# Opening the program with the input projection, and dealing page compression's other products out between its chunks

## The chip, the cores and the metric

One core of one Trainium2 chip runs the whole program. The metric is the device time of one execution in microseconds (us), the median over several runs. TensorE (PE in the profile) multiplies; VectorE (DVE), ScalarE (ACT) and GpSimd (POOL) work on elements; SyncE (SP) and the queues of the other engines start DMA transfers. The five engines run their own instruction streams and meet at semaphores. TensorE's clock has two levels, 2.4 GHz (granted clock 1.00 in the profile) and 1.2 GHz (0.50).

## The reference

One inference step of a two-layer decoder, for a prompt of 512 tokens and 8 single sample tokens together (T = 520 columns everywhere, D = 1024). Layer 0 mixes tokens with native sparse attention, layer 1 with a gated linear recurrence; each layer ends in a SwiGLU network. The part that matters here is how layer 0 begins:

```
q, kv, gates = split(rms_norm(x) @ nsa_w_in)          # 1024 -> 2608 columns
z  = blocks of 64 raw K (or V) rows + position weights # prompt: 8 blocks, sample: 8 x 32 blocks from paged cache
kc = silu(z @ w1) @ w2                                  # 4096 -> 64 -> 64 for each block and head
s_c = q . kc * scale + bias(distance)                   # scores of the prompt over its 8 blocks, softmax
```

The distance bias is one table of 32 buckets x 16 heads, looked up by token distance.

## The kernel before

All products are in float32 or in pairs of rounded parts: a weight tile and an activation are each cut into a high part and a rest, and three products take the place of one. `linear` (L137) runs a projection over weight tiles of 512 KB that lie in a ring of four slots. For each tile ACT copies the high part (`cut`, L280), DVE subtracts it (L312), PE does 8 x 6 matmuls of 260 columns (`one`, L400), and DVE moves the result out of one of four PSUM banks. In the first tile PE also adds up the squares of x (L413) for the RMS norm, whose inverse root is wanted before the first result moves out: two-bank lookahead lets PE do tile 1 meanwhile, and it waits for the inverse before tile 2. SP loads tile n+4 when the rest of tile n is cut, and after each of the first 16 such loads runs `beside`, which fetches two pages of the compression cache (`first_chunks`). The projection has 21 tiles.

Ahead of it stands a block of its own, `bias_rows` (L1154). SP loads the one-hot rows, the table, x in one piece, small constants, and the first four weight tiles; PE makes the 16 x 1024 bias rows with two float32 matmuls (L1188); DVE scales them; ACT stores them to DRAM. A block ends for all engines together, and SP ends it only when x and the constants are in. Then the projection's block starts. There SP first runs `early` (`spread_bias`, L2596): it waits for the stored rows and copies them 128 times with a shift, 5 MB within DRAM, in one transfer.

Page compression is the block `compress` (L1199). The cache's 128 pages are taken as 8 chunks of 16 pages, 256 KB each, in two slots of 4 MB. Chunks 0 and 1 are in when the block starts. Chunk g+2 goes into the slot of chunk g: SP (9 pages) and POOL (7 pages) wait for `chunk_done` of chunk g and then issue the page loads one after another (`load_chunk`, L1250). A chunk is 128 float32 matmuls of 64 columns on 64-column weights (L1295), each two records in the trace. Beside the chunks PE has other products here: turning gates and values (L1327, L1330, L1310), the prompt's blocks against w1 (`prompt`, L1303, 17 columns, 2 x 128 records), the block bias (L1339, 14 matmuls of 16 columns), the second products (L1347, L1349, at the end L1381 and L1384), the block scores (L1361, 32 matmuls of 16 columns on 128-column weights), the turned probabilities (L1368) and the sample bias (`far`, L1318, six). The order on PE is written out by hand: chunk 0, 1, gates, new values, both prompt products, block bias, values of two tiles, chunk 2, second products and the other values, chunk 3, all block scores, chunk 4, turned probabilities, far 0 and 1, chunk 5, far 2 and 3, chunk 6, far 4 and 5, chunk 7, the last second products. The attention block follows.

Later, between the first network and the recurrence's projection, ACT takes the last inverse root of the norm (`end.root(act, 4, ...)`, L542, at the end of `Layer.scalar`), then cuts the high part of tile 2 (L280). DVE waits for the root (`rooted`), cuts the rest (L312), and moves tile 0 out (L2071), which frees the bank that tile 2 needs.

Of the kernel before, what the change touches and what calls it, by code (L numbers as in the profile page):

```python
# [20 lines left out]
P = 128  # L21
# [30 lines left out]
SKEW = SEQ + P  # L52
FINE = (0, 1, 2, 4, 8, 16)
# [83 lines left out]
def linear(c, name, w, n_units, subs, kcs, src, evac, nxt, scale=None, beside=None, norm=None, early=None, late=None, work=None, unrolled=False, first=None, start=0):  # L137
# [19 lines left out]
    with ExitStack() as ctx:  # L157
# [19 lines left out]
        def rounds(eng, cut, first_done=None, tail=None):  # L177

            def step(i, s):
                if cut is not None:  # L180
                    cut(i, s)
                if isinstance(i, int) and i == 0 and s == 0:
                    if first_done is not None:
                        first_done()
                    return
                if isinstance(i, int) and i == 0 and s == 1 and tail is not None and norm is not None:
                    tail()
                r, q = (i, s - 1) if s else (i - 1, RING - 1)
                if q % subs == subs - 1:
                    evac(eng, ps, q // subs, r, ready)  # L190

# [51 lines left out]
        def _(sp):  # L243
            if first is not None:
# [31 lines left out]
        def _(act):  # L276
# [5 lines left out]
            def cut_source():  # L282
                if post is not None:
                    root(1)
                for k in range(kcs):
                    if post is not None:
                        act.wait_ge(x_new[k % 2], k // 2 + 1)
                    act.activation(xh[:, k, :], src[:, k, :], ACT.Copy,
# [9 lines left out]

            if first is not None:
# [71 lines left out]
        def _(pool):  # L371
            if post is not None:
# [9 lines left out]
        def _(pe):  # L382
# [33 lines left out]
            def add_squares(k):  # L416
                pe.wait_ge(squared, k + 1)
                token_sums(ps[2], sq[:, k % 2, :], k == 0, k == kcs - 1).then_inc(added, 1)
# [189 lines left out]
class Layer:  # L608
# [108 lines left out]
    def scalar(self, act):  # L717
# [101 lines left out]
        end.root(act, 4, COLS[1])  # L819
# [13 lines left out]
    def vector(self, dve):  # L833
# [97 lines left out]
        end.mean(dve, own_end, 1)  # L931

# [221 lines left out]
def bias_rows(c, d, tabs, oh, R, loaded, row_out):  # L1154

    nc = c.nc
    with ExitStack() as ctx:
        ps = [ctx.enter_context(nc.psum_tensor(f"row_ps{j}", [P, 512], F32)) for j in range(2)]
        made, moved = [nc.alloc_semaphore(f"row_{n}") for n in ("products", "scaled")]
        oh_in = nc.alloc_semaphore("row_onehot_loaded")  # L1160
        block = ctx.enter_context(nc.Block())

        @block.sync
        def _(sp):
            sp.dma_start(oh, d["onehot_rows"][:, 0]).then_inc(oh_in, 16)
            sp.dma_start(tabs[:, :], d["tabs"]).then_inc(oh_in, 16)
            for dst, src in loaded[1]:
                sp.dma_start(dst, d[src]).then_inc(loaded[0], 16)
            for s in range(RING):
                load_tile(sp, c, d["nsa_w_in"], s, s, KC)  # L1170
            sp.wait_ge(loaded[0], 16 * len(loaded[1]))

        @block.scalar
        def _(act):
            act.wait_ge(moved, 2)
            act.dma_start(d["bias_scratch"], R).then_inc(row_out, 16)

        @block.gpsimd
        def _(pool):
            pool.memset(c.ones[:, :], 1.0)  # L1180
            for s in range(RING):
                pool.sem_inc(c.psum_free[s], 1)

        @block.tensor
        def _(pe):
            pe.wait_ge(oh_in, 32)
            for j in range(2):
                pe.matmul(ps[j][0:16, :], tabs[:, 0:16], oh[:, j * 512:(j + 1) * 512], start=True, stop=True)\  # L1188
                  .then_inc(made, 1)

        @block.vector
        def _(dve):
            for j in range(2):
                dve.wait_ge(made, j + 1)
                dve.tensor_scalar(R[:, j * 512:(j + 1) * 512], ps[j][0:16, :], HD ** 0.5, None, ALU.mult).then_inc(moved, 1)


def compress(c, d, at, tabs, first_in, w1, w1_in, kcBD, v_rep, skew_out):
# [7 lines left out]
    with ExitStack() as ctx:  # L1206
# [47 lines left out]
        def _(sp):  # L1254
# [17 lines left out]
            sp.wait_ge(skew_out, 16)  # L1272
# [11 lines left out]
        def _(pe):  # L1284
            def chunk(g):
# [11 lines left out]
                mm.then_inc(chunk_done[s], 1)  # L1297
# [9 lines left out]
            def values(i, bank):  # L1307

                for j, u in enumerate((SV_U, SV_U + 1, WV_U, WV_U + 1)):
                    mm = pe.transpose(bank[:, j * P:(j + 1) * P], HT[:, u, i * P:(i + 1) * P], c.ident[:, :])  # L1310
                mm.then_inc(tok_turned, 1)
# [8 lines left out]

            pe.wait_ge(w1_in, 16)
            pe.wait_ge(first_in, 16 * 2 * CH)
            chunk(0)
            chunk(1)
# [10 lines left out]
            pe.wait_ge(onehots, 32)  # L1335
            for x in range(PBLK + 2 * (TILES - 1)):

                first = BLOCK * (2 * (TILES - 1) - x) - (BLOCK - 1) + 511
                mm = pe.matmul(b[2][:, x * 16:(x + 1) * 16], oh[:, first:first + P], tabs[:, 0:16], start=True, stop=True)  # L1339
            mm.then_inc(blocks_biased, 1)  # L1340
            values(0, b[5])
            pe.wait_ge(gates_out, 1)
            values(1, b[3])
            chunk(2)
# [6 lines left out]
            pe.wait_ge(new_out, 1)  # L1351
            values(2, b[4])
            pe.wait_ge(tok_out, 1)
            values(3, b[5])
            chunk(3)
            pe.wait_ge(bias_out, 1)
            pe.wait_ge(kc_ready, 1)
            for i in range(TILES):
                for u in range(8):
                    col = (i * 8 + u) * 16  # L1360
                    mm = pe.matmul(b[2][:, col:col + 16], c.XW[:, u, i * P:(i + 1) * P],  # L1361
                                   kcBD[:, u // REP].rearrange("p g n -> p (g n)"), start=True, stop=True)
            mm.then_inc(scores, 1)
            chunk(4)
            pe.wait_ge(probs, 1)
            pe.wait_ge(tok_out, 4)
# [4 lines left out]
            far(0)  # L1371
            far(1)
            chunk(5)
            far(2)
            far(3)
            chunk(6)
            far(4)
            far(5)
            chunk(7)
# [8 lines left out]
        def _(act):  # L1388
# [9 lines left out]
            for j, (first, n) in enumerate(FAR):  # L1398
                act.wait_ge(far_biased, j + 1)
                act.activation(at.bias[:, first:first + n], b[4 + j % 2][:, 0:n], ACT.Copy).then_inc(far_out, 1)  # L1400
            for s in range(2):
                act.wait_ge(chunk_done[s], NCH // 2)
            for kv in range(2):
                act.activation(hid[:, kv, 0:512], ps_c[kv][:, :], ACT.Silu, bias=pe_w[:, kv:kv + 1]).then_inc(hidden, 1)

# [1137 lines left out]
def program(nc, d):  # L2543

    with ExitStack() as top:
# [19 lines left out]
        with ExitStack() as nsa:  # L2565
# [12 lines left out]
            bias_rows(c, d, tabs, carve(HT[0:N_BUCKETS + 1, 4:6, :].rearrange("p u t -> p (u t)"), 0, 1024),  # L2578
                      carve(HT[0:16, 11:13, :].rearrange("p u t -> p (u t)"), 0, 1024),
# [180 lines left out]
```

## Time and profile before

| | |
|---|---|
| median of 3 runs | 1723.29 us (1721.01 to 1731.25) |
| the profiled execution: time, span | 1718.65 us, 1717.0 us |
| mean granted TensorE clock | 0.965 |
| PE busy | 1614.6 us, 94% of the span |
| DVE, POOL, ACT busy | 47%, 33%, 32% |
| read from and written to HBM | 217.8 MB, 23.8 MB |

"Busy" is the time in which an engine had an instruction under way, whatever the clock. The first products of the projection stand at 15.7 us, page compression reaches from 149.1 to 273.9 us, and the rest is attention, two networks and the recurrence. In a timeline row the bracket tells how long the engine was idle ahead of the row, and what ended it; "issue" means that nothing shown in the profile held it.

### The profile page before, as it was taken

What the parts mean: (1) busy time and instruction counts of PE and PEld (TensorE: products, weight loads), DVE (VectorE), ACT (ScalarE), POOL (GpSimd) and SP (SyncE); (2) the same over time, 40 slices, a digit from 0 to 9 for tenths busy, and PEclk for the clock granted to TensorE, in tenths of its full rate; (3) what the DMA queues carried; (4) which work ended last, traced back from release to release, by engine and by line L of the source; (5) the groups of instructions that cost most, each with busy time, mean ns of one, the idle gap of its engine ahead of it and who ended that gap; (6) DMA issues with size and microseconds to landing.
All of it is one profiled execution on the core that took longest, in us unless ns stands there. A gap on an engine that the chain in (4) does not pass through costs nothing. (4 is left out here: it accounts for less than half of the span.)

```text
span 1717.0 us, 40632 instructions
## 1 busy us (share of the span) xinstructions
PE 1614.6 (94%) x16686; PEld 1502.3 (87%) x16686; DVE 808.6 (47%) x1350; ACT 551.0 (32%) x1040; POOL 564.8 (33%) x505
## 2 busy tenths in 40 slices
PE   6998997798989999999999899999989999999996
PEld 5998985555669999999999889989889999999995
DVE  4333114556555543444237676766447444343235
ACT  3110003456554322222235433333344222222242
POOL 0001222567633433443104333333014444343013
PEclk9999778899999999999999899999989999999998
DMA  9654687777752122223234234433221222223242
GB/s 285 211 187 178 217 293 276 287 239 228 218 193 79 59 88 87 97 86 119 89 132 145 83 113 96 141 111 100 75 89 60 76 96 86 97 86 118 94 160 84
DMA packets 86264, 238.50 MB, mean 139 GB/s; under 512 B 18109, under 2 KB 20847, under 8 KB 84545
## 3 DMA queue, kind: packets, MB, share of 16 engines
q1 hardware_dynamic: 80786, 221.63, 39.2%
q0 software_dynamic: 3392, 11.02, 1.8%
q10 hardware_dynamic: 1936, 3.74, 0.6%
q8 instruction: 108, 1.77, 0.4%
q14 instruction: 42, 0.34, 0.1%
HBM read 217.81 MB, written 23.77 MB: 141 GB/s over the span
## 5 line engine op out<-in xcount | busy, mean ns | idle before, releaser
L846 DVE TENSOR_TENSOR layer_w_lo<-ring,layer_w_hi 128x1024 fp32r<-128x1024 f32 (+1 forms) x138 | 225.5, 1634 | 265.8 <-ACT layer_w_hi L728 265.8
L993 PE MATMUL layer_ps<-layer_x_hi,layer_w_hi 128*128 128x260 f32 x1312 | 269.0, 284 | 2.7 <-DVE layer_w_lo L846 2.7
L993 PE MATMUL layer_ps<-layer_x_hi,layer_w_lo 128*128 128x260 f32 x1312 | 268.3, 284 | 0.0
L993 PE MATMUL layer_ps<-layer_x_lo,layer_w_hi 128*128 128x260 f32 x1312 | 267.8, 284 | 0.0
L728 ACT ACTIVATE layer_w_hi<-ring 128x1024 fp32r<-128x1024 f32 (+1 forms) x138 | 160.9, 1167 | 221.8 <-PE layer_ps L993 206.4
L993 PE MATMUL layer_ps<-layer_h_lo,layer_w_hi 128*128 128x260 f32 x960 | 217.6, 287 | 10.9 <-DVE layer_h_lo L852 10.9
L993 PEld LDWEIGHTS layer_ps<-layer_x_hi,layer_w_hi 128*128 128x128 f32 x1312 | 204.6, 189 | 4.3 <-DVE layer_w_lo L846 2.9
L993 PEld LDWEIGHTS layer_ps<-layer_x_hi,layer_w_lo 128*128 128x128 f32 x1312 | 204.7, 189 | 0.0
L993 PEld LDWEIGHTS layer_ps<-layer_x_lo,layer_w_hi 128*128 128x128 f32 x1312 | 204.0, 189 | 0.1
L993 PE MATMUL layer_ps<-layer_h_hi,layer_w_hi 128*128 128x260 f32 x704 | 172.8, 286 | 4.8 <-DVE layer_w_lo L846 4.8
L993 PEld LDWEIGHTS layer_ps<-layer_h_lo,layer_w_hi 128*128 128x128 f32 x960 | 160.8, 192 | 12.0 <-DVE layer_w_lo L846 11.8
L993 PE MATMUL layer_ps<-layer_h_hi,layer_w_lo 128*128 128x260 f32 x704 | 170.2, 282 | 0.0
L1803 POOL TENSOR_SCALAR arena<-arena 128x128 f32<-128x128 f32 (+3 forms) x128 | 137.3, 1089 | 78.5 <-DVE arena L1934 78.3
L487 POOL TENSOR_TENSOR layer_h_hi<-mixer_out 128x520 f32 (+1 forms) x44 | 59.1, 1344 | 290.4 <-DVE mixer_out L476 290.3
L476 DVE TENSOR_TENSOR mixer_out<-layer_ps,rstd 128x520 f32<-128x520 f32 x88 | 61.5, 699 | 189.8 <-PE layer_ps L993 188.2
L993 PEld LDWEIGHTS layer_ps<-layer_h_hi,layer_w_hi 128*128 128x128 f32 x704 | 120.4, 188 | 7.1 <-DVE layer_w_lo L846 6.5
L993 PEld LDWEIGHTS layer_ps<-layer_h_hi,layer_w_lo 128*128 128x128 f32 x704 | 120.5, 188 | 0.0
L400 PE MATMUL layer_ps<-layer_x_hi,layer_w_hi 128*128 128x260 f32 x480 | 103.8, 298 | 3.7 <-DVE rec_f L2071 2.9
L480 ACT ACTIVATE mixer_out<-mixer_out 128x520 f32<-128x520 f32 x44 | 28.1, 639 | 224.3 <-DVE mixer_out L476 224.3
L1772 ACT ACTIVATE arena<-arena 128x128 f32<-128x128 f32 (+3 forms) x128 | 70.6, 553 | 90.2 <-DVE arena L1922 80.4
L400 PE MATMUL layer_ps<-layer_x_hi,layer_w_lo 128*128 128x260 f32 x480 | 97.7, 285 | 0.5 <-issue 0.5
L1250 POOL DMA_DIRECT2D arena<-in_cache_cmp x42 | 22.8, 544 | 227.4 <-issue 227.4
(319 smaller groups left out, 3055.0 us busy)
## 6 DMA issues: line engine op xcount, KB each, us to landing
ring<-in_w_gu SPq DMA_DIRECT2D x88, 512.0 KB, 3.5
ring<-in_w_down SPq DMA_DIRECT2D x48, 704.0 KB, 4.1
arena<-in_cache_cmp SPq DMA_DIRECT2D x86, 256.0 KB, 5.1
ring<-in_hgrn_w_in SPq DMA_DIRECT2D x32, 512.0 KB, 3.7
X<-in_slc_kv SPq DMA_DIRECT2D x48, 256.0 KB, 3.3
ring<-in_nsa_w_in SPq DMA_DIRECT2D x21, 512.0 KB, 3.7
arena<-in_cache_cmp POOLq DMA_DIRECT2D x42, 256.0 KB, 5.5
ring<-in_slc_kv SPq DMA_DIRECT2D x40, 256.0 KB, 3.0
```

What stands on the lines that cost most here:

```text
L400: last = pe.matmul(ps[j][:, h, 0:TH], wt[:, s % 2, a], xt[:, x, h * TH:(h + 1) * TH], start=(sub == 0 and k == 0 and part == 0), stop=(sub ...
L476: eng.tensor_tensor(pairs((g_t if is_g else a_t)[:, m, :]), ps[j][:, :, 0:TH], pairs(c.rstd[:, :]), ALU.mult).then_inc(c.psum_free[j], 1)
L480: eng.activation(a_t[:, m, :], a_t[:, m, :], ACT.Silu).then_inc(a_act[m], 1)
L487: eng.tensor_tensor(hi, a_t[:, m, :], g_t[:, m, :], ALU.mult).then_inc(made, 1)
L728: act.activation(self.w_hi[slot][:, 0:kcs * P], c.ring[:, s, 0:kcs * P], ACT.Copy).then_inc(c.hi_cut[s], 1)
L846: dve.tensor_tensor(self.w_lo[slot][:, 0:kcs * P], c.ring[:, s, 0:kcs * P], self.w_hi[slot][:, 0:kcs * P].bitcast(F32), ALU.subtract).then ...
L993: mm = pe.matmul(bank[:, h, 0:TH], wt[slot][:, a], xt[:, x, COLS[h]], start=start and part == 0, stop=stop and part == 2)
L1250: eng.dma_start(slot(g % 2)[:, x, :], d["cache_cmp"][bass.ds(page, 1)].rearrange("o p n -> p (o n)"))\
L1772: act.activation(E[h][s % 4][:, col:col + w], Sb[h][s % 2][:, col:col + w], ACT.Exp, bias=nm[:, k:k + 1], scale=-1.0, accum_out=rs[:, k:k ...
L1803: ins = pool.tensor_scalar(E[h][s % 4][:, col:col + w], E[h][s % 4][:, col:col + w], sc[:, k:k + 1], None, ALU.mult)
```

## The change

The block `bias_rows` is gone. `linear` takes an `opening` whose parts run inside the projection's own block: x comes in eight pieces, after the norm weights and the first weight tile and ahead of tiles 1 to 3; the one-hot rows, the table and small constants are issued on ACT's queue; ACT's first activation is an empty one; PE makes the bias rows ahead of tile 2, in the bank of tile 3; DVE scales them and ACT stores them around the move of tile 1. The spread to DRAM is cut into eight parts, put beside steps 2 to 5 and 7 to 10 of SP's loop. The weights w1 come as before, at the loop's end.

In `compress` PE's order becomes: chunk 0, gates, new values, chunk 1, `prompt(0)`, chunk 2, `prompt(1)`, chunk 3 with the block bias dealt out in it, a second product, chunk 4 with the values of two tiles, a second product, chunk 5 with the other values, chunk 6 with the 32 block scores, far 0 and 1, chunk 7 with far 2 and 3, turned probabilities, far 4 and 5, the last second products. "Dealt out" means one call after every four chunk matmuls (32 places in a chunk). ACT copies far 4 and 5 after its last silu. Between network and recurrence the last root is put behind ACT's cut of tile 2.

```diff
+SPREAD_STEPS = (2, 3, 4, 5, 7, 8, 9, 10)
 # linear: rounds.step
+                if isinstance(i, int) and i == 0 and s == 2 and opening is not None:
+                    opening.rows(eng, ps[RING - 1])
 # linear: rounds_beside, n == 1
                     if cut is not None:
                         cut(0, start)
+                    if eng is nc.scalar:
+                        first.last_root(eng)
 # linear: cut_source, sync, scalar, gpsimd call opening.source_in, .sync, .scalar, .gpsimd; tensor:
                 if s == 2 and norm is not None:
                     pe.wait_ge(inverse, means)
+                if s == 2 and opening is not None:
+                    opening.tensor(pe, ps[RING - 1])
                 one(s, 0)
 # Layer.scalar
-        end.root(act, 4, COLS[1])
+class Opening:
+    def sync(self, sp):
+        sp.dma_start(c.nw[:, :, :, :], d["norm_w"]).then_inc(self.norm_in, 16)
+        load_tile(sp, c, d["nsa_w_in"], 0, 0, KC)
+        for k in range(KC):
+            sp.dma_start(c.X[:, k, :], d["x"][:, k, :]).then_inc(self.x_in[k], 16)
+        for s in range(1, RING):
+            load_tile(sp, c, d["nsa_w_in"], s, s, KC)
+        sp.wait_ge(self.pages_in, 16)
+    def scalar(self, act):
+        act.dma_start(self.oh, d["onehot_rows"][:, 0]).then_inc(self.rows_in, 16)
...
+        act.wait_ge(self.ones_made, 1)
+        act.activation(c.scrap[:, :], c.ones[:, 0:1], ACT.Copy)
+        act.wait_ge(self.norm_in, 16)
+    def tensor(self, pe, bank):
+        pe.wait_ge(self.rows_in, 32)
+        for j in range(2):
+            pe.matmul(bank[0:16, j, :], self.tabs[:, 0:16], self.oh[:, j * 512:(j + 1) * 512], start=True, stop=True)\
+              .then_inc(self.made, 1)
+    def rows(self, eng, bank):
+        if eng is c.nc.vector:
+            for j in range(2):
+                eng.wait_ge(self.made, j + 1)
+                eng.tensor_scalar(self.R[:, j * 512:(j + 1) * 512], bank[0:16, j, :], HD ** 0.5, None, ALU.mult)\
+                   .then_inc((self.moved, c.psum_free[RING - 1])[j], 1)
+        if eng is c.nc.scalar:
+            eng.wait_ge(self.moved, 1)
+            eng.wait_ge(c.psum_free[RING - 1], 1)
+            eng.dma_start(self.d["bias_scratch"], self.R).then_inc(self.row_out, 16)
 # compress, tensor: chunk
+                        if kv and t == TP - 1:
+                            mm.then_inc(chunk_done[s], 1)
+                        if beside is not None and t % 2:
+                            beside(kv * (TP // 2) + t // 2)
...
             chunk(0)
-            chunk(1)
             pe.wait_ge(gated, 1)
...
+            chunk(1)
             pe.wait_ge(pairs_ready, 1)
             prompt(0)
+            chunk(2)
             prompt(1)
+            chunk(3, block_bias)
...
+            chunk(4, first_values)
...
+            chunk(5, last_values)
+            chunk(6, block_scores)
+            pe.wait_ge(tok_out, 4)
+            far(0)
+            far(1)
+            chunk(7, far_biases)
             pe.wait_ge(probs, 1)
...
             far(4)
             far(5)
             pe.wait_ge(hidden, 1)
 # first_chunks
+                if step in SPREAD_STEPS:
+                    spread_bias(sp, SPREAD_STEPS.index(step))
 # spread_bias(sp, part): waits for row_out in part 0; each part copies 2 of the 16 heads
```

## Rows read from the trace of the kernel before

**Rows 1.** The page, first part: busy time and share of the span.
```profile
PE 1614.6 (94%) x16686; PEld 1502.3 (87%) x16686; DVE 808.6 (47%) x1350; ACT 551.0 (32%) x1040; POOL 564.8 (33%) x505
```

**Rows 2.** Busy time by stretch: length, engines' busy us (instructions), granted clock, DMA share, GB/s.
```profile
0.00:20.00 20.00, 7.88 (x20) 4.35 (x21) 4.68 (x6) 6.13 (x9) 0.41 (x5) 1.00 0.84 300
...
40.00:60.00 20.00, 20.00 (x168) 20.00 (x167) 5.77 (x6) 3.19 (x3) 0.00 (x0) 1.00 0.72 260
```

**Rows 3.** The timeline of the opening: start us, us, engine, line, what.
```profile
3.42 3.59 PE L1188 MATMUL row_ps<-HT,tabs 33*16 33x512 f32 x4 [3.42 <-DMA tabs<-in_tabs]
...
11.21 1.28 ACT L280 ACT_TABLE_LOAD   x1 [11.21 <-PEq L1157]
12.51 1.06 ACT L280 ACTIVATE nsa_in_w_hi<-ring 128x1024 fp32r<-128x1024 f32 x1
...
15.71 0.77 PE L400 MATMUL nsa_in_ps<-nsa_in_x_hi,nsa_in_w_hi 128*128 128x260 f32 x2 [8.70 <-DVE nsa_in_x_lo L359]
...
31.77 3.40 DVE L332 RECIPROCAL rstd<-rstd 128x520 f32<-128x520 f32 x1
...
38.29 0.48 PE L400 MATMUL nsa_in_ps<-nsa_in_x_hi,nsa_in_w_hi 128*128 128x260 f32 x2 [1.43 <-DVE nsa_in_w_lo L312]
```

**Rows 4.** DMA issues of the first 40 us: what, queue, count, KB each, median us to landing.
```profile
bias_skew<-bias_scratch SPq DMA_DIRECT2D x1, 5120.0 KB, 26.5
```

**Rows 5.** The prompt products (L1303) by stretch: PE, PEld busy, clock, DMA share, GB/s.
```profile
168.87:170.50 1.63, 1.63 (x51) 1.59 (x51) 1.00 1.05 395
172.25:173.80 1.55, 1.55 (x54) 1.55 (x54) 1.00 1.11 374
173.80:182.18 8.38, 8.38 (x159) 8.34 (x155) 0.50 1.03 355
```

**Rows 6.** The chunk products (L1295) by stretch, same columns.
```profile
190.16:194.30 4.14, 4.14 (x78) 4.14 (x80) 0.50 0.00 0
194.40:199.60 5.20, 5.20 (x182) 5.16 (x178) 1.00 0.01 3
201.14:208.76 7.62, 7.62 (x256) 7.55 (x256) 1.00 0.89 291
```

**Rows 7.** The block scores (L1361) by stretch, same columns.
```profile
209.86:211.30 1.44, 1.44 (x13) 1.44 (x13) 1.00 1.03 401
211.40:222.00 10.60, 10.60 (x51) 10.60 (x50) 0.50 1.04 387
```

**Rows 8.** The timeline of PE in page compression, and its last DVE row.
```profile
165.78 2.25 PE L1295 MATMUL cmp_ps<-arena,X 128*64 128x64 f32 x69 [1.16 <-issue]
...
182.18 6.15 PE L1339 MATMUL cmp_b<-tabs,T_bias 33*128 33x16 f32 x28
...
200.17 1.04 PE L1310 MATMUL cmp_b<-ident,HT 128*128 128x128 f32 x8
...
240.48 2.32 PE L1295 MATMUL cmp_ps<-arena,X 128*64 128x64 f32 x73 [1.39 <-issue]
242.73 1.98 PE L1318 MATMUL cmp_b<-sample_bias,tabs 33*128 33x512 f32 x4
247.28 9.99 PE L1295 MATMUL cmp_ps<-arena,X 128*64 128x64 f32 x256 [2.57 <-DMA arena<-in_cache_cmp]
...
259.08 1.61 PE L1295 MATMUL cmp_ps<-arena,X 128*64 128x64 f32 x46 [0.62 <-DMA arena<-in_cache_cmp]
261.55 6.62 PE L1295 MATMUL cmp_ps<-arena,X 128*64 128x64 f32 x210 [0.86 <-issue]
...
273.19 0.69 DVE L1475 COPY vcS<-cmp_b 128x512 f32<-128x512 f32 x1 [1.04 <-PE cmp_b L1384]
```

**Rows 9.** The timeline where the recurrence's projection starts.
```profile
967.78 0.42 ACT L542 ACTIVATE rstd<-rstd 128x260 f32<-128x260 f32 x1 [3.99 <-DVE rstd L532]
968.11 1.04 ACT L280 ACTIVATE layer_w_hi<-ring 128x1024 fp32r<-128x1024 f32 x1
...
971.22 0.47 PE L400 MATMUL layer_ps<-layer_x_hi,layer_w_hi 128*128 128x260 f32 x2 [2.89 <-DVE rec_f L2071]
```

More of the change, by code:

```diff
@@ L134, in repeat, with linear @@
             yield i
-def linear(c, name, w, n_units, subs, kcs, src, evac, nxt, scale=None, beside=None, norm=None, early=None, late=None, work=None, unrolled=False, first=None, start=0):
+def linear(c, name, w, n_units, subs, kcs, src, evac, nxt, scale=None, beside=None, norm=None, early=None, late=None, work=None, unrolled=False, first=None, start=0, opening=None):
     nc = c.nc
@@ L243, in _ @@
         def _(sp):
+            if opening is not None:
+                opening.sync(sp)
             if first is not None:
@@ L287, in cut_source @@
                         act.wait_ge(x_new[k % 2], k // 2 + 1)
+                    if opening is not None:
+                        opening.source_in(act, k)
                     act.activation(xh[:, k, :], src[:, k, :], ACT.Copy,
@@ L297, in root @@
                 act.activation(c.rstd[:, :], c.rstd[:, :], ACT.Sqrt).then_inc(rooted, 1)
+            if opening is not None:
+                opening.scalar(act)
             if first is not None:
@@ L371, in _ @@
         def _(pool):
+            if opening is not None:
+                opening.gpsimd(pool)
             if post is not None:
@@ L417, in add_squares @@
                 pe.wait_ge(squared, k + 1)
+                if opening is not None and k == 0:
+                    pe.wait_ge(opening.ones_made, 1)
                 token_sums(ps[2], sq[:, k % 2, :], k == 0, k == kcs - 1).then_inc(added, 1)
@@ L931, in vector, with last_root @@
         end.mean(dve, own_end, 1)
+    def last_root(self, act):
+        self.end.root(act, 4, COLS[1])
     def rooted(self, dve):
@@ L1151, in load_bias_tiles @@
     eng.dma_start(at.T_bias[:, u % 2], src).then_inc(at.bias_in[u % 2], 16)
[L1154 to L1186, printed above, removed]
-            for j in range(2):
[L1188 to L1195, printed above, removed]
@@ L1284, in _, with chunk @@
         def _(pe):
-            def chunk(g):
+            def chunk(g, beside=None):
                 s = g % 2
@@ L1319, in far, with block_bias, first_values, last_values @@
                           start=True, stop=True).then_inc(far_biased, 1)
+            LINES = PBLK + 2 * (TILES - 1)
+            def block_bias(x):
+                if x == 0:
+                    pe.wait_ge(onehots, 32)
+                if x < LINES:
+                    first = BLOCK * (2 * (TILES - 1) - x) - (BLOCK - 1) + 511
+                    mm = pe.matmul(b[2][:, x * 16:(x + 1) * 16], oh[:, first:first + P], tabs[:, 0:16], start=True, stop=True)
+                    if x == LINES - 1:
+                        mm.then_inc(blocks_biased, 1)
+            def first_values(x):
+                if x == 0:
+                    pe.wait_ge(gates_out, 1)
+                if x < 8:
+                    value(x // 4, b[5 - x // 4 * 2], x % 4)
+            def last_values(x):
+                if x == 0:
+                    pe.wait_ge(new_out, 1)
+                if x == 4:
+                    pe.wait_ge(tok_out, 1)
+                if x < 8:
+                    value(2 + x // 4, b[4 + x // 4], x % 4)
+            def block_scores(x):
+                if x == 0:
+                    pe.wait_ge(bias_out, 1)
+                    pe.wait_ge(kc_ready, 1)
+                i, u = x // 8, x % 8
+                mm = pe.matmul(b[2][:, x * 16:(x + 1) * 16], c.XW[:, u, i * P:(i + 1) * P],
+                               kcBD[:, u // REP].rearrange("p g n -> p (g n)"), start=True, stop=True)
+                if x == 31:
+                    mm.then_inc(scores, 1)
+            def far_biases(x):
+                if x in (23, 30):
+                    far(2 + x // 30)
             pe.wait_ge(w1_in, 16)
@@ L1397, in _, with far @@
             act.activation(S, S, ACT.Exp).then_inc(expd, 1)
-            for j, (first, n) in enumerate(FAR):
+            def far(j):
+                first, n = FAR[j]
                 act.wait_ge(far_biased, j + 1)
                 act.activation(at.bias[:, first:first + n], b[4 + j % 2][:, 0:n], ACT.Copy).then_inc(far_out, 1)
+            for j in range(4):
+                far(j)
             for s in range(2):
@@ L1404, in _ @@
                 act.activation(hid[:, kv, 0:512], ps_c[kv][:, :], ACT.Silu, bias=pe_w[:, kv:kv + 1]).then_inc(hidden, 1)
+            for j in range(4, 6):
+                far(j)
         @block.vector
```

85 lines of the change are left out of this document (39 added, 46 removed).

## The prediction

> **What bounds the kernel now.** I read the page's busy shares first: PE is busy for 94% of the span, no other engine for half of it [rows 1]. So a part of the change can only pay where PE idles or where its clock is down. The table by stretch shows where: in the first 20 us PE is busy for 7.9 us, from 40 us on for 20 of 20 [rows 2]. The rest of the projection is PE's own work and moves along with its start. The timeline of the opening says why PE starts at 15.71 us: ACT enters the projection's block at 11.21 us, loads a table for 1.28 us, and cuts the first tile at 12.51 us; cut, rest and first source piece take the 3.2 us to the first matmul [rows 3].
>
> Page compression has two troubles. One is the clock. Prompt products run at 28.7 ns a record (1.55 us / 54) while 1.00 is granted and at 52.7 ns (8.38 / 159) after it fell to 0.50, 4.9 us behind their start [rows 5]; block scores at 111 ns (1.44 / 13) and 208 ns (10.60 / 51) [rows 7]; chunk products at 29.8 ns (7.62 / 256) and 53.1 ns (4.14 / 78) [rows 6]. The clock fell in stretches of 16 or 17 columns and rose again in chunk products. The other trouble is the pages. A load asked for at the end of one chunk is in so late that 16.3 us pass before PE can begin the chunk after the next: chunk 5 ends at 242.7, chunk 7 begins at 259.1, both waits being ended by DMA [rows 8]. Between chunk 3 and chunk 5 the old order has 13 us of scores (208.8 to 222.0 [rows 6, 7]) and all of chunk 4, so no wait stands there.
>
> **The opening.** Removed: the wait of one block for x and all constants. The table load moves under the DMA wait. The first cut now needs only tile 0 and the norm weights. Lower bound of its start: small transfers are in at 3.42 us [rows 3]; 0.5 MB at the 300 GB/s of the first 20 us [rows 2] are 1.8 us more, so 5.2 us. Upper bound: the one-hot rows, the constants and the first piece of x share the queues, 0.5 MB more, 6.9 us. I take 5.6 us, near the lower end because tile 0 is second in its queue: 12.51 - 5.6 = **6.9 us earlier**, between 5.6 and 7.3. The pieces of x (0.27 MB, 0.9 us each by that rate) come faster than ACT and PE use them (PE takes the eight from 15.71 us on, and the reciprocal of their squares begins at 31.77 [rows 3]), so nothing waits for them.
>
> Added to PE: four records of bias rows ahead of tile 2. They took 3.59 us at the start [rows 3], at 1.2 GHz by their pace; at 2.4 GHz half, 1.8 us. PE idles for 1.43 us there before, behind the reciprocal of 3.40 us [rows 3]; that cover is used up, and **0.3 us** lie on the path. If the cover went, the price would be 1.8 us. DVE's two scalings and ACT's store stand behind the move of tile 1 and ahead of the cut of tile 3; PE is in tile 2 for 5.7 us then (48 of the 168 records in 20 us of [rows 2]), and cut and rest (1.1 and 1.2 us) with about 3 us of added waiting still fit. ACT's waits for the scaled rows hold up only that cut.
>
> Moved on SP: the spread, 5 MB, that took 26.5 us to land beside the first weight tiles [rows 4], becomes eight pieces between the loads of tiles 6 to 14. Part 0 waits for the stored rows, some 5 us at worst, and behind it on SP stand two pages and tile 7; PE wants tile 7 about 20 us later. By bytes a step of 5.7 us has 1.05 MB of tile and pages and 0.66 MB of spread, 1.7 MB against the 300 GB/s x 5.7 = 1.7 MB of [rows 2]: just enough, with a ring of four tiles as a buffer. Cost 0, and at most 2 us if the queue falls behind. Sum of the opening: 6.9 - 0.3 = **6.6 us**, between 3.5 and 7.2.
>
> **Page compression**, in times of the old trace. Chunk 1 ended at 168.0 and ends at 168.9 now, since the gates (0.8 us, to 168.87 [rows 5, 8]) go ahead of it. `prompt(0)` is half of the 13.3 us that both took [rows 5, 8], between 5.4 us (128 x 28.7 ns and the gap of 1.7 us seen between the first two stretches [rows 5]) and 6.7; I take 6: 174.9. Chunk 2's pages, asked for at 157, are in by 173. A chunk during loads takes 9.1 us at full clock with its gap of 0.9 (chunk 7), 10.0 us where the clock was down at its start (chunk 6) [rows 8]; I take 9.7: 184.6. `prompt(1)`: 190.6.
>
> Chunk 3 with the block bias decides. The bias is 28 records, 6.15 us at the low clock [rows 8], 3.1 us if it halves. At full clock chunk 3 takes 9.1 + 3.1 = 12.2 us. If `prompt(1)` has brought the clock down, the first 112 chunk records and the bias take 5.9 + 6.2 us, the other 144 about 6 (low for some 4 us, as after 190.16 [rows 6]): 18.1 us. I take the second, because the nearest row is the bias itself, which ran directly behind prompt products and wholly at the low level. Chunk 3 ends at 208.7, as before (208.8 [rows 6]).
>
> From there the page loads set the pace: 208.7 + 16.3 = 225.0 for chunk 5's start (chunk 4 with its eight turned values ends near 220, so **a new wait of some 5 us** stands before chunk 5). Chunk 5 starts at the low clock as chunk 6 did: 10.0 + 1.0 for its values [rows 8] = 236.0. Chunk 6 with the 64 score records: 256 x 29.8 ns + 64 x 111 ns = 14.7 us, 0.5 for a gap: 251.2; bounds 14.7 and 26.9 (all at the low prices). Far 0 and 1: 2.0 [rows 8], 253.2; chunk 7's pages are in at 252.3. Chunk 7 with far 2 and 3: 9.1 + 2.0 = 264.3. The tail from chunk 7's end to the block's end is 273.9 - 268.2 = 5.7 us [rows 8], the turned probabilities and far 4 and 5 lying beside ACT's silu: 270.0 against 273.9, **3.9 us**. Softmax on DVE, which the turned probabilities wait for, has all of chunk 7 as cover.
>
> **The root.** Old order: root at 967.78, cut of 1.04 us, rest, move, PE at 971.22 after 2.89 us idle [rows 9]. ACT was idle for 3.99 us ahead of the root [rows 9], so the cut fits there, and DVE can begin when the root is done: **1.1 us**; 0 if the tile is not free yet.
>
> **Sum.** 6.6 + 3.9 + 1.1 = 11.6 us. The profiled execution, 1718.65 us (span 1717.0 and 1.65 around it), would become 1707.0; it lies 4.64 us under the median, so on the median's scale 1723.3 - 11.6 = **1711.7 us**.
>
> **A rule against the rows.** In [rows 7] PE was busy for the whole 12 us and the clock fell nevertheless. The Trainium skill (TensorE: Matmul & The Clock Gate, "Loop structure matters more than you think") says that matmuls that follow one another keep the clock up and that long waits for DMA let it fall. The rows agree on waits (chunk 6 began low behind 2.57 us of idling [rows 8]) and disagree on back-to-back work; by the rule the first rival below, 1703 us, is the likeliest case, by the rows it is not.
>
> **Rivals.**
> Clock up throughout: prompt products are now short stretches between chunks, and dealt-out products never stand alone. Prompts 5.4 each, chunk 2 9.1, chunk 3 12.2: it ends at 201.0. Then 217.3 for chunk 5, 10.1 for it, 15.2 for chunk 6, 2.0, 11.1 for chunk 7, 5.7: 261.4. Gain 12.5 in place of 3.9: **1703 us**. For it: chunks alone raised the clock again in under 5 us [rows 6]. Against: it fell 4.9 us into prompt products [rows 5]. Chance 0.22.
>
> No gain in compression: the load distances and a chunk 6 that is half at the low clock (+6 us) eat what the shorter products give, or the spread costs 2 us. The stage gains about -1, the total is 6 to 7: **1717 us**. For it: 16.3 us per two chunks is a floor of 3 x (16.3 + 10) us from chunk 1 on, which reaches to 253 with the tail. Chance 0.20.
>
> Slower: the mixture is too thin for the high level, and from `prompt(0)` to chunk 7 all runs at 1.2 GHz. Chunks at 256 x 53.1 = 13.6 us, chunk 3 19.8, chunk 6 26.9, values and far at double price: the block ends near 300 in place of 273.9, 26 us lost. With 7.7 us from elsewhere: **1741 us**. It turns the sum to a loss from about 40% of the way between 270 and 300 on. Against it: the chunk that began at 0.50 at 190.16 had 1.00 from 194.40 on [rows 6]. Chance 0.05. Main case 0.53, of its own range 1707 to 1716.
>
> **Numbers.** Range 1702 to 1719: it leaves out the slower case, the upper end of the second and the lower end of the first. A measurement can tell 1%, 17 us, from no change; faster than that (below 1706.1) is the first rival and a sliver of the main case, 0.23; slower than that 0.03; within 0.74.
>
> **What would show it.** First 260-column matmul at 8 to 10 us; PE idle ahead of tile 2 near 0; projection without PE gaps between 30 and 90 us. In compression: clock at the end of `prompt(1)` and in chunk 3 (0.50 in my case, 1.00 in the first rival); a DMA wait of about 5 us ahead of chunk 5; scores in chunk 6 at 1.00. Wrong if PE starts later than 11 us, if chunk 6 takes over 20 us, or if a wait for pages stands ahead of chunk 0 or for weights in the projection.

## The result and the profile after

The changed kernel takes 1737.88 us (median of 12 runs, 1731.96 to 1745.88), the kernel before 1723.0 us (12 runs, 1717.02 to 1731.25). The ratio is 1.009, 95% interval 1.007 to 1.011: slower by 15 us, where 1711.7 was forecast, and outside the range.

The profiled execution has a span of 1738.5 us, 21.5 more than before. The opening gives 6.0 us, page compression costs 27.5, and from its end to the end of the program both kernels take the same: 1738.5 - 295.35 = 1443.2 against 1717.0 - 273.88 = 1443.1. The medians are only 14.9 us apart: the profiled execution before lies 4.4 us under its median, the one now (1740.32 us) 2.4 us over it. Some 7 of the 21.5 us are therefore the spread between executions, and two traces can't tell in which stage they lie.

Compression is counted from PE's first chunk product to the end of DVE's last copy: 149.31 to 273.88 before [rows 8], 143.29 to 295.35 now, so 124.6 and 152.1 us. The first chunk products, before and now:

```profile
149.31 9.40 PE L1295 MATMUL cmp_ps<-arena,X 128*64 128x64 f32 x315 [1.21 <-PEq L157]
143.29 7.68 PE L1337 MATMUL cmp_ps<-arena,X 128*64 128x64 f32 x256 [1.21 <-PEq L158]
```

The page's first part, in the columns of [rows 1]: PE's share is 94% as before, but 26.8 us more of busy time went into the same 16686 matmuls. The table by stretch follows, in those of [rows 2].

```profile
PE 1641.4 (94%) x16686; PEld 1518.2 (87%) x16686; DVE 809.2 (47%) x1350; ACT 550.8 (32%) x1041; POOL 564.3 (32%) x505
```

By stretch, PE is busy for 11.1 of the first 20 us in place of 7.9, and without a break in the projection while the spread lies beside it:

```profile
0.00:20.00 20.00, 11.10 (x54) 10.11 (x55) 6.14 (x8) 10.71 (x17) 0.41 (x5) 1.00 0.77 277
40.00:60.00 20.00, 20.00 (x169) 20.00 (x167) 6.57 (x7) 3.18 (x3) 0.00 (x0) 1.00 0.94 340
60.00:80.00 20.00, 20.00 (x169) 20.00 (x168) 6.54 (x8) 4.24 (x4) 0.00 (x0) 1.00 0.85 309
```

The timeline of the opening, against [rows 3]: the table load now stands ahead of the first tile's arrival, the first cut at 5.69 us, the first product at 8.90, the bias rows at 30.43 without idle time in front.

```profile
3.10 1.28 ACT L1205 ACT_TABLE_LOAD   x1 [3.10 <-issue]
5.69 1.06 ACT L287 ACTIVATE nsa_in_w_hi<-ring 128x1024 fp32r<-128x1024 f32 x1 [1.10 <-DMA ring<-in_nsa_w_in]
8.90 0.78 PE L413 MATMUL nsa_in_ps<-nsa_in_x_hi,nsa_in_w_hi 128*128 128x260 f32 x2 [8.90 <-DVE nsa_in_x_lo L370]
...
30.43 1.89 PE L1223 MATMUL nsa_in_ps<-HT,tabs 33*16 33x512 f32 x4
```

Page compression, by stretch (length, then busy us and instructions of PE, PEld, DVE, ACT, POOL, then granted clock, DMA share, GB/s): chunk 3 with the bias; chunk 4; chunk 5; chunk 6 in its first 6 us and in the rest; far 0 and 1; chunk 7 with far 2 and 3.

```profile
185.22:207.60 22.38, 22.38 (x289) 20.16 (x287) 1.11 (x5) 1.73 (x3) 2.51 (x5) 0.55 0.48 167
207.90:218.80 10.90, 10.90 (x266) 9.31 (x265) 1.63 (x4) 0.00 (x0) 3.75 (x7) 1.00 0.79 267
224.58:240.29 15.71, 15.71 (x272) 12.91 (x272) 2.58 (x4) 0.00 (x0) 1.61 (x3) 0.63 0.58 213
240.29:246.20 5.91, 5.91 (x86) 5.15 (x82) 0.00 (x0) 0.00 (x0) 2.47 (x5) 1.00 0.72 217
246.30:273.06 26.76, 26.76 (x231) 23.20 (x231) 0.00 (x0) 0.00 (x0) 1.18 (x3) 0.50 0.55 208
273.06:276.70 3.64, 3.64 (x5) 1.17 (x4) 2.73 (x5) 1.11 (x2) 0.00 (x0) 0.50 0.00 0
276.77:288.40 11.63, 11.63 (x261) 9.96 (x260) 1.81 (x5) 1.42 (x3) 0.00 (x0) 0.84 0.01 3
```

PE has an instruction under way for the whole of every stretch, so no wait for another engine stands here. Chunk 6 takes 33.0 us: 32.8 from its first score (240.29) to 273.06, and 0.24 for the eight chunk records ahead of that. Its products, each kind alone at the high clock, came to 14.7. The timeline of PE shows one place after another, 8 chunk records and 2 score records each, and the fall of the clock; the wait ahead of chunk 5 stands in it too, and DVE's last copy.

```profile
224.58 0.70 PE L1337 MATMUL cmp_ps<-arena,X 128*64 128x64 f32 x8 [5.27 <-DMA arena<-in_cache_cmp]
...
225.61 0.70 PE L1337 MATMUL cmp_ps<-arena,X 128*64 128x64 f32 x8
...
245.24 0.40 PE L1402 MATMUL cmp_b<-kcBD,mixer_out 128*128 128x16 f32 x2
245.56 0.45 PE L1337 MATMUL cmp_ps<-arena,X 128*64 128x64 f32 x8
245.95 0.40 PE L1402 MATMUL cmp_b<-kcBD,mixer_out 128*128 128x16 f32 x2
246.27 0.65 PE L1337 MATMUL cmp_ps<-arena,X 128*64 128x64 f32 x8
...
271.35 0.61 PE L1402 MATMUL cmp_b<-kcBD,mixer_out 128*128 128x16 f32 x2
271.89 0.70 PE L1337 MATMUL cmp_ps<-arena,X 128*64 128x64 f32 x8
272.52 0.61 PE L1402 MATMUL cmp_b<-kcBD,mixer_out 128*128 128x16 f32 x2
...
294.66 0.69 DVE L1550 COPY vcS<-cmp_b 128x512 f32<-128x512 f32 x1 [1.03 <-PE cmp_b L1452]
```

From one score pair to the next are 0.705 us (245.24 to 245.95) while the clock is up and 1.17 us (271.35 to 272.52) while it is down. By the prices of [rows 6, 7] the ten records cost 8 x 29.8 + 2 x 111 ns = 0.460 us, or 8 x 53.1 + 2 x 208 = 0.841. So a place costs **0.245 us** at the high clock and **0.33 us** at the low one beyond its products, for the change to the other kind of product and back.

The root, against [rows 9]: PE's idle time ahead of tile 2 fell from 2.89 to 1.85 us.

```profile
993.16 0.47 PE L413 MATMUL layer_ps<-layer_x_hi,layer_w_hi 128*128 128x260 f32 x2 [1.85 <-DVE rec_f L2146]
```

### The profile page after: what moved, and what is told of

The parts are those of the page before. It is cut to its first block and busy times, and to the rows that moved or that the text cites. A ratio compares the mean times of both kernels' runs of the same rounds, so it can differ in the third digit from the quotient of the medians.

```text
span 1738.5 us, 40638 instructions
## 1 busy us (share of the span) xinstructions
PE 1641.4 (94%) x16686; PEld 1518.2 (87%) x16686; DVE 809.2 (47%) x1350; ACT 550.8 (32%) x1041; POOL 564.3 (32%) x505
## 3 DMA queue, kind: packets, MB, share of 16 engines
q8 instruction: 108, 1.77, 0.4%
## 5 line engine op out<-in xcount | busy, mean ns | idle before, releaser
L1013 PE MATMUL layer_ps<-layer_h_lo,layer_w_hi 128*128 128x260 f32 x960 | 217.4, 287 | 10.7 <-DVE layer_h_lo L868 10.7
L1337 PE MATMUL cmp_ps<-arena,X 128*64 128x64 f32 x2048 | 92.7, 253 | 10.7 <-DMA arena<-in_cache_cmp 5.3
```

The source lines that it names most:

```text
L1013: mm = pe.matmul(bank[:, h, 0:TH], wt[slot][:, a], xt[:, x, COLS[h]], start=start and part == 0, stop=stop and part == 2)
L1337: mm = pe.matmul(ps_c[kv][g2 * HD:(g2 + 1) * HD, g * CH * 4:(g + 1) * CH * 4], w1[:, kv, t, :], slot(s)[:, :, col:col + 4], start=t == 0, ...
```

## Experiments

Two theories stood at the start. **S**: the extra price is paid where PE switches between products of the chunk's shape (128 rows on weights of 64 columns) and products of another shape, 62 places in the new order; the slow stretch then brings the clock down too. **O**: it is the new order itself, in which chunks run while pages load and pages are asked for at worse times. Theory D came later. Ratios are to the kernel before on the same chip in the same batch; its median there was 1733.1 us for e1 to e4, 1721.9 for e5 to e8 and 1723.5 for e9, so times of different batches are compared by ratio only. Stage times are from one profiled execution each. What follows compression varied from 1437 to 1454 us over the nine profiled experiments, so a difference of a few us in a stage need not show in the ratio.

**e1_blocks.** The changed kernel, nothing dealt out in chunks 3 to 6; far 2 and 3 stay in chunk 7.

```
-chunk(3, block_bias)
+chunk(3)
+for x in range(LINES): block_bias(x)
 # likewise first_values behind chunk 4, last_values behind chunk 5, block_scores behind chunk 6
```

> The changed kernel with its new order of chunks, but block bias, values and scores stand as blocks behind chunks 3, 4, 5 and 6 and are not dealt out between their products. Theory S (a product on 128-column weights between chunk products on 64-column weights costs 0.24 us or more beyond its price alone, each time, and the thinner work then brings the clock down): chunk 6 with its scores falls from 32.8 us to 9 to 11 plus 13, chunk 3 with the bias from 22.4 to about 16; the stage falls from 152 to about 125 us, the program to 1709 to 1715 us. Theory O (the new order is at fault: a chunk that ends later asks for its pages later, and the wait of 5.3 us ahead of chunk 5 shows it): the order is kept, so the stage stays above 143 us and the program above 1729.

Ratio 0.9955 (0.9933 to 0.9976). Compression 134.2 us, between the two expectations and 17.9 less than the changed kernel's 152.1, so dealing out is the larger part of the loss. But 134.2 is 11 more than the old order has in the next experiment: O holds a part. The waits of PE in compression (us in total, times, longest) show which:

```profile
PE cmp_ps L1337 <- issue: 10.2, 6, 2.8
PE cmp_ps L1337 <- DMA arena<-in_cache_cmp: 5.8, 2, 4.7
PE cmp_b L1348 <- issue: 2.6, 1, 2.6
PE cmp_b L1402 <- issue: 1.3, 1, 1.3
```

**e2_opening.** The new opening, the spread in eight parts and the moved root, with `compress` as before.

```
 # compress: as in the kernel before, but
+sp.wait_ge(skew_out, 16 * len(SPREAD_STEPS))
```

> The changed kernel with the page compression of the kernel before: the opening, the spread in eight parts and the later root alone. Theories S and O both: page compression starts 6.0 us earlier as in the changed kernel and takes its old 125 us; the root's 1.0 us was given back in the recurrence: 1716 to 1718 us on the scale of 1723. If the spread's traffic in the projection, or the opening, were what costs: above 1723.

Ratio 0.9935 (0.9909 to 0.9961): 11 us faster, 7 to 16. Compression begins at 142.84 and takes 123.2 us; "issue" stands in it for 5.6 us (4.9 ahead of chunk products, 0.7 elsewhere) and the pages for 3.9. The forecast of 6.6 + 1.1 lies in the interval.

```profile
PE cmp_ps L1337 <- issue: 4.9, 4, 2.0
PE cmp_ps L1337 <- DMA arena<-in_cache_cmp: 3.9, 1, 3.9
```

**e3_halves.** The changed kernel, all dealt out as it was, but each bias and score product as two of 64 columns, so that a score product has the chunk's shape.

```
-mm = pe.matmul(b[2][:, x * 16:(x + 1) * 16], c.XW[:, u, i * P:(i + 1) * P], ...
+for g2 in range(2):
+    mm = pe.matmul(b[2][g2 * HD:(g2 + 1) * HD, x * 16:(x + 1) * 16],
+                   c.XW[:, u, i * P + g2 * HD:i * P + (g2 + 1) * HD], ...
 # the same for block_bias
```

> The changed kernel, still dealt out, but each block bias product and each block score product is split into two products on 64-column weights that write the two halves of the partitions, as the chunk products do (values stay whole). Theory S with the weight shape as its reason: a place in chunk 6 takes 0.36 to 0.45 us in place of 0.71 (clock up) and 1.17 (clock down), chunk 6 12 to 15 us and the clock stays at 1.00 in it, chunk 3 11 to 14; program 1706 to 1713. If any product that breaks into the row of chunk products costs the same, whatever its weights: a place costs as much or more (twice as many breaks), chunk 6 over 30 us, the program 1737 or more.

Ratio 0.9927 (0.9897 to 0.9957). Compression 128.4 us, 23.7 less. Chunk 6, first by the timeline of PE:

```profile
235.91 0.24 PE L1405 MATMUL cmp_b<-kcBD,mixer_out 128*64 128x16 f32 x4
236.00 0.43 PE L1337 MATMUL cmp_ps<-arena,X 128*64 128x64 f32 x8
236.26 0.24 PE L1405 MATMUL cmp_b<-kcBD,mixer_out 128*64 128x16 f32 x4
```

and by stretch:

```profile
235.91:247.00 11.09, 10.31 (x354) 10.17 (x350) 0.00 (x0) 0.00 (x0) 3.77 (x7) 1.00 0.84 288
```

A place takes 0.35 us, half of 0.705, with two records more. The shape's surcharge is gone, and the clock stays at 1.00 in the 11 us shown. Chunk 3 took 19.4 us (184.49 to 203.90) where 11 to 14 were expected. It ran at the low clock behind `prompt(1)`, and the bias halves keep a surcharge of 0.3 us: 33 rows on 64 columns are still another shape than the chunk's 128 rows, and their places took 0.955 us at the low clock, where the eight chunk records (0.425) and the four halves alone (56 took 3.17 us in the next experiment, so 0.23) make 0.65.

**e4_old_halves.** e2_opening with the same halves, standing alone as in the old order.

```
 # e2_opening, and in its loops of block bias and block scores:
+for g2 in range(2):
+    mm = pe.matmul(b[2][g2 * HD:(g2 + 1) * HD, ...], ... 64 columns of the weights ...)
```

> The opening alone (page compression in its old order, other products standing by themselves), with block bias and block scores split into products on 64-column weights. By the price of the prompt products, which have such weights (28.7 ns a record with the clock up, 52.7 down), the scores are 128 records of that, 3.7 to 6.7 us in place of 13.3, and the bias 1.6 to 3 in place of 6.2: 9 to 13 us less than the opening alone, 1704 to 1708. If a product costs by its count and not by its weights' columns: 1717 or more.

1713.65 us, ratio 0.9884 (0.9836 to 0.9932), compression 119.4 us. The scores alone, in the timeline of PE:

```profile
201.12 3.06 PE L1406 MATMUL cmp_b<-kcBD,mixer_out 128*64 128x16 f32 x99
206.92 1.68 PE L1406 MATMUL cmp_b<-kcBD,mixer_out 128*64 128x16 f32 x27 [2.74 <-issue]
```

128 records of 64 columns take 4.8 us of PE time (126 are in the trace), the 64 records of 128 columns took 12.0 [rows 7]. The first 99 ran at a granted clock of 1.00, 31 ns each against 111; those in the second row at 0.50, 55 ns each (1.48 us / 27) against 208 [rows 7]. Compression is only 3.8 us shorter than in e2_opening, where 9 to 13 were expected: "issue" rose from 5.6 to 13.9 us, which is most of what the products gave.

**e5_grouped.** The changed kernel, whole products, same share of them in each chunk, but dealt out four places at a time: 8 switches to another shape in chunk 6 in place of 32. This sets S against **D**, by which the share of thin products in a chunk brings the clock down, however they lie.

```
-if beside is not None and t % 2:
-    beside(kv * (TP // 2) + t // 2)
+if beside is not None and t % 8 == 7:
+    for x in range(4):
+        beside(kv * (TP // 2) + t // 2 - 3 + x)
```

> The changed kernel, with the same products dealt out in fewer places: one call of four places after every 16 chunk matmuls, 8 in a chunk in place of 32. Theory S (each switch between products of chunk shape, 128 rows on 64 columns, and another shape costs 0.24 us at the high clock and 0.33 at the low one, and the slow stretch that it makes then lets the clock fall): bias and scores lose 46 of their 62 breaks, chunk 6 takes 7.6 + 7.1 + 8 x 0.24 + 0.5 = 17 us in place of 32.8, at most 21 if the clock falls late in it; compression about 135 us in place of 152, time about 1721. Rival D (it is the share of 16-column products in the chunk that lets the clock fall, however they are grouped): the clock falls about 6 us into chunk 6 again and chunk 6 takes 27 us or more, compression 145 or more, time 1731 or more.

1710.09 us, ratio 0.9929 (0.9899 to 0.9959). Compression 127.7 us. Chunk 6, in the table by stretch, and one group of it in the timeline of PE:

```profile
234.74:251.20 16.46, 16.46 (x324) 15.72 (x319) 0.00 (x0) 0.00 (x0) 3.77 (x7) 1.00 0.90 314
```

```profile
235.69 1.06 PE L1403 MATMUL cmp_b<-kcBD,mixer_out 128*128 128x16 f32 x8
236.69 1.15 PE L1337 MATMUL cmp_ps<-arena,X 128*64 128x64 f32 x32
237.77 1.06 PE L1403 MATMUL cmp_b<-kcBD,mixer_out 128*128 128x16 f32 x8
```

16.5 us (with the first 32 chunk records) where S gave 17 and D 27 or more, and the clock didn't fall in it. A group of 32 + 8 records takes 2.08 us (235.69 to 237.77); alone they are 0.95 + 0.89. That leaves 0.24 us for one switch there and back, the same as a place of two score records paid: the price hangs on the switch, not on the number of products. In chunk 3, at the low clock, 32 + 8 records took 3.72 against 1.70 + 1.76 alone: 0.26. Its chunk 3 still ran at 0.53 and took 20.2 us, behind `prompt(1)`.

**e6_light_blocks.** e1_blocks with a quarter of each page of chunks 2 to 7.

```
-eng.dma_start(slot(g % 2)[:, x, :], d["cache_cmp"][bass.ds(page, 1)].rearrange("o p n -> p (o n)"))
+eng.dma_start(slot(g % 2)[:, x, 0:P], d["cache_cmp"][bass.ds(page, 1)].rearrange("o p n -> p (o n)")[:, 0:P])
```

> The kernel e1_blocks (new order, nothing dealt out), with chunks 2 to 7 loading only the first 128 of the 512 columns of each page; three quarters of those pages' values are left out of the result, the instructions of all engines stay the same. Theory O (the idle 'issue' stretches inside the chunks, 14.1 us in e1_blocks, and the waits for pages, 5.8 us, are made by the page loads that run beside them): 'issue' falls under 4 us, the waits for pages to about 0, compression from 134.2 to about 117 us. Rival I (the stretches belong to the chunks' own instruction stream): 'issue' stays at 10 us or more, only the waits for pages go, compression about 128.

Compression 114.7 us in place of 134.2. PE's waits:

```profile
PE cmp_ps L1337 <- DMA arena<-in_cache_cmp: 4.7, 2, 2.8
PE cmp_ps L1337 <- issue: 2.2, 2, 1.6
PE cmp_b L1348 <- issue: 0.4, 1, 0.4
```

The instructions are the same and "issue" falls from 14.1 to 2.6 us: the page loads make it, as O said. The waits for pages went to 4.7 only, not to about 0. From the end of chunk 4 to the start of chunk 6 pass 12.7 us in place of 16.8, since a part of that distance doesn't depend on the bytes: SP starts its nine page loads one after another, here from 204.9 to 214.5 us, and in the kernel before from 243.6 to 252.4, ahead of chunk 7. Only the landing of a load got shorter, by the median from 5.5 us to 2.3.

```profile
L1292 SPq DMA_DIRECT2D arena<-in_cache_cmp x9: 333/333/785, 204.9 to 214.5; - x9
L1250 SPq DMA_DIRECT2D arena<-in_cache_cmp x9: 337/338/338, 243.6 to 252.4; - x9
```

**e8_light_dealt.** The changed kernel with the same quarter pages.

```
 # the changed kernel, with the edit of e6_light_blocks
```

> The changed kernel, with chunks 2 to 7 loading only the first 128 of the 512 columns of each page; three quarters of those pages' values are left out of the result. Theory S (the price of a place lies in the switch of shapes): a place in chunk 6 (8 chunk records, 2 score records) still takes about 0.70 us at the high clock and 1.17 at the low one, the clock falls in chunk 6 again, and compression loses only its wait for pages (5.3 us) and its idle 'issue' stretches: 152 to about 140 us. Rival O (the page loads slow the supply of instructions, and a place is dear for that): a place falls to 0.24 + 0.24 = 0.48 us, chunk 6 takes under 20 us, compression about 125.

Compression 138.6 us. Chunk 6 in the table by stretch:

```profile
225.53:229.76 4.23, 4.23 (x60) 3.66 (x60) 0.00 (x0) 0.00 (x0) 1.60 (x3) 1.00 0.28 81
229.76:260.09 30.33, 30.33 (x262) 26.31 (x261) 0.00 (x0) 0.00 (x0) 2.14 (x4) 0.50 0.32 111
```

Places take 0.705 and 1.17 us as with whole pages, and the clock falls again: chunk 6 is 34.6 us. So the page loads have no part that shows in the price of a place.

**e7_prompt_apart.** One part of the new order on top of e4_old_halves: `prompt(0)` and two tiles' values ahead of chunk 2, `prompt(1)` and the bias behind it.

```
 prompt(0)
+pe.wait_ge(gates_out, 1)
+values(0, b[5])
+values(1, b[3])
+chunk(2)
 prompt(1)
...
-values(0, b[5])
-pe.wait_ge(gates_out, 1)
-values(1, b[3])
-chunk(2)
```

> The kernel e4_old_halves (new opening, old order, bias and scores in halves of 64 columns, compression 119.4 us, 1713.65 us), with one part of the new order: prompt(0) and the first two tiles' values before chunk 2, prompt(1) and the block bias after it. Chunk 2 starts about 171 in place of 182.8, so chunk 4's pages are asked for about 10 us earlier. Theory P (the prompt's move is good by itself and the losses of the new order lie in the later steps): chunk 7 starts 5 us earlier, compression about 114, time about 1709. Rival O (every chunk that runs while pages load has about 2 us more of idle 'issue' and the waits for pages only move): compression 119 to 124, time 1714 to 1718.

1703.2 us, ratio 0.9892 (0.9858 to 0.9927). Compression 117.7 us, 1.7 less than e4_old_halves: between the two expectations. By ratio the program is not faster than e4_old_halves (0.9884). Chunk 4 starts at 203.6 in place of 208.4, but the wait ahead of the last pages grew, and chunk 7 starts only 2.7 us earlier, at 245.2.

```profile
203.58 6.90 PE L1337 MATMUL cmp_ps<-arena,X 128*64 128x64 f32 x229
...
245.22 9.29 PE L1337 MATMUL cmp_ps<-arena,X 128*64 128x64 f32 x256 [4.75 <-DMA arena<-in_cache_cmp]
```

**e9_far_late.** e7_prompt_apart with turned probabilities, far 0 and 1 behind chunk 5 and far 2 to 5 behind chunk 6.

```
 chunk(4)
+chunk(5)
...
 far(0)
 far(1)
-chunk(5)
-far(2)
-far(3)
 chunk(6)
-far(4)
-far(5)
+for j in range(2, 6):
+    far(j)
 chunk(7)
```

> The kernel e7_prompt_apart (compression 117.65 us; there far 0 and 1 take 3.8 us at the low clock between chunk 4 and 5, and chunk 7 waits 4.75 us for its pages), with one more move: the turned probabilities and far 0 and 1 go behind chunk 5, far 2 to 5 behind chunk 6, so that chunk 5 follows chunk 4 at once. Theory P (what paces the end is the time at which the last pages are asked for, at the end of chunk 5): chunk 5 ends about 4.5 us earlier, chunk 7 starts at about 240 to 241 in place of 245.2, and the far products stand in the waits for pages; compression about 113 us, ratio to the kernel before about 0.986. Rival O (the earlier loads slow the chunks beside them, or chunk 5 now waits for its own pages): chunk 7 starts at 244 or later, compression 117 us or more, ratio 0.989 or more.

1706.25 us, ratio 0.9900 (0.9869 to 0.9931), no better than e7_prompt_apart; compression 118.7 us. The rival was right: chunk 5 now waited 1.89 us and chunk 6 1.15 us for their own pages, "issue" in the chunks rose from 8.5 to 12.9 us, and chunk 7 started at 248.2.

## Why the prediction was wrong

**The step that failed** is "Chunk 6 with the 64 score records: 256 x 29.8 ns + 64 x 111 ns = 14.7 us". It adds prices that were read from products standing among their own kind, and PE did not keep them when the kinds alternate. Of the 18.3 us between 14.7 and 33.0, the switches there and back at 32 places make 32 x 0.245 = 7.8 us and the low clock 23 places x (1.17 - 0.705) = 10.7. Both disappear when the switches do: in e5_grouped with the shape kept and the places grouped (16.5 us), where the eight switches that are left cost 0.24 us each, and in e3_halves with the shape changed (13.4 us from the first score on, a 2.2 us "issue" gap included). That the switches are the cause is shown; why the array needs the time, and why the clock falls behind them, is not. The Trainium skill (TensorEngine Tiling (Array Packing), "Key Properties") says that a change of the array's tiling mode, and not just of the tile, drains the engine; it gives no time. The runs agree: 128 rows on 128 columns, 33 on 128 and 33 on 64 all cost it beside 128 on 64, and 128 on 64 beside 128 on 64 does not.

The bounds failed with it. "All at the low prices", 26.9 us, was no upper bound, because the price of the mixture itself was in no row of before, and nothing above the dearest separate prices was allowed for.

**Chunk 3** (18.1 forecast, 22.4 measured): the low clock was foreseen and came (0.55); 14 places with a switch of 0.3 us are 4.2 of the 4.3 us that lack.

**Chunk 5** (11.0 forecast, 15.5 measured, to 240.05): the wait ahead of it was foreseen (5 us, 5.27 measured) and that it starts at the low clock too. Its eight places with a value took 1.035 us each, all at the low clock, where eight chunk records and a value alone make 0.67 (8 x 53.1 ns and 1.97 us / 8, the values before at 188.26); that is 2.9 us of switches. The rest is the clock, which stayed down for 11.4 us, and rose when the chunk products had stood alone for 3 us:

```profile
224.58:236.00 11.42, 11.42 (x131) 8.69 (x132) 2.58 (x4) 0.00 (x0) 1.61 (x3) 0.50 0.79 293
236.00:240.05 4.05, 4.05 (x142) 4.05 (x142) 0.00 (x0) 0.00 (x0) 0.00 (x0) 0.99 0.00 0
```

Far 0 and 1, 2.0 forecast, took 3.8 at the low clock that chunk 6 left. Chunk 4 (10.9 us) came out right by luck: its eight places at the high clock took 0.64 us each where the products alone make 0.37 [rows 6, 8], 2.2 us of switches, and in return no gap and no low clock stood in it. Chunk 7 with far 2 and 3 took 11.7 against 11.1.

**The rival of the slower side** named the right outcome, 1741 us, with 0.05 of the chance. Its mechanism, a mixture too thin for the high level, was half of it: the clock fell in chunk 6 only behind the switches, and the same share of thin products in groups ran at 1.00 throughout. The rule weighed in the prediction (the Trainium skill, TensorE: Matmul & The Clock Gate, "Loop structure matters more than you think") does not foresee it: no wait for DMA stands in PE's rows between 224.58 and the fall of the clock at 246.3. But this is weaker evidence against it than the scores before [rows 7]. A third of each place (0.245 of 0.705 us) is switch, the weight loads (PEld) were under way for only 5.15 of the 5.91 us ahead of the fall, and whether the array worked during a switch no row tells.

**The new order itself** costs 11 us against the old (e1_blocks against e2_opening, 134.2 and 123.2), which the forecast had as a gain of 3.9 with the dealing out. It had given a chunk one gap of 0.9 us; with chunks running beside page loads, "issue" grew from 5.6 to 14.1 us and the waits for pages from 3.9 to 5.8, together 10.4. The 16.3 us between the end of a chunk and the start of the chunk after the next, which the forecast took as the time that the pages need, are for more than half the nine loads that SP starts one after another (8.8 us from the first to the last, and 5.5 us median for one to land); sharing them out over more queues was not tried.

**The opening** was right: the first product came 6.8 us earlier (6.9 forecast), compression began 6.0 us earlier (6.6); the bias rows took 1.89 us (1.8; the 3.59 us before were put down to 1.2 GHz by their pace, but the granted clock stands at 1.00 in the first 20 us [rows 2], so why they took about double stays open), and tile 2 started 6.0 us earlier, so the 0.8 us lost lie ahead of it. The spread costs the projection nothing, PE being busy for 20.00 of 20 us at a DMA share of 0.94. **The root** gave 1.04 us of idle time (1.1 forecast), which the total does not show: it is smaller than the spread of what follows compression.

## What to carry to other kernels

Before small matmuls are dealt out among others, compare rows and columns of their weights: where these differ, add a price for every switch there and back (here 0.24 to 0.27 us at 2.4 GHz, 0.26 to 0.36 at 1.2) or group them, and where they can be cut to the same shape, cut them. A price read from a run of equal products is no bound for a mixture. Where a reordering puts PE's work beside heavy loads, count PE's "issue" gaps as a cost that comes with it. Where many loads are started one after another, count the starts before the bytes.

## What the hardware showed beyond that

The "issue" gaps belong to the supply of instructions, as far as the runs show. Between two gaps lie exactly 128 products in many places (in e9_far_late, PE's timeline in chunk 4), each with its weight load, so 256 instructions; the instruction queue, in the list of queues on the page of the changed kernel (packets, MB, share), moves packets of 16 KB (1.77 MB / 108); and the gaps shrink with the page bytes (e6_light_blocks).

```profile
208.69 3.95 PE L1337 MATMUL cmp_ps<-arena,X 128*64 128x64 f32 x128 [0.23 <-issue]
215.16 1.03 PE L1337 MATMUL cmp_ps<-arena,X 128*64 128x64 f32 x27 [2.53 <-issue]
```

```profile
q8 instruction: 108, 1.77, 0.4%
```

The Trainium skill (Runtime: NRT & Kernel Launch, "Instruction fetch mechanics") says that instructions come in blocks of 16 KiB, 256 of them, over a DMA queue of the engine's own, and calls the cost mostly hidden. The size agrees; the cost does not: a block took up to 3.0 us of PE's time beside page loads (e9_far_late, the gap ahead of 156.41, at a DMA share of 0.90). That the blocks wait behind the pages' packets was not tried by itself.

The best kernels of the runs are the new opening with the old order and scores and bias in halves, with the prompt products apart (e7_prompt_apart, 1703.2 us, ratio 0.9892) or without that step (e4_old_halves, 1713.65 us, ratio 0.9884). Their intervals overlap, so which of the two is faster is not shown.
